# An encoder layer on one core: loads around the out projection spread, the second product's block split early, the sums of h given to GpSimd

## What is computed

```python
def encoder_layer(x, w_in, w_fourier, sink_logits, w_out, ln_mix_g, ln_mix_b, w_ff1, w_ff2, ln_ffn_g, ln_ffn_b):
    proj = x @ w_in
    ...
    heads = jnp.concatenate([fourier_mix(u, w_fourier),
                             windowed_attention(q, k, v, sink_logits)], axis=-1)
    x = layer_norm(DEEPNORM_ALPHA * x + heads @ w_out, ln_mix_g, ln_mix_b)
    h = jnp.square(jax.nn.relu(x @ w_ff1))
    x = layer_norm(DEEPNORM_ALPHA * x + h @ w_ff2, ln_ffn_g, ln_ffn_b)
    return x
```

## Time and profile before

| | before |
|---|---|
| median of three runs | 2422.47 us |
| the profiled execution | 2422.82 us, span 2421.2 us |
| TensorE busy | 2362.3 us (98%) |
| VectorE busy | 1568.6 us (65%) |
| ScalarE busy | 1101.7 us (46%) |
| GpSimd busy | 182.9 us (8%) |
| out projection | about 622 to 862 us of the span |
| up projection, groups 0, 1, 2 | 863.7, 1099.4 and 1336.1 us to 1649 us |

### The profile page before, as it was taken

One profiled execution on the slowest core, in us unless ns is written; L12 is line 12 of the kernel. 1 busy time (PEld: TensorE's weight loads), 2 busy tenths in 40 slices (PEclk: granted clock), 3 DMA queues, 4 the chain that ended last, 5 costly groups with the idle time before them and its releaser, 6 DMA issues. The chain is left out here.

```text
span 2421.2 us, 34853 instructions
## 1 busy us (share of the span) xinstructions
PE 2362.3 (98%) x12028; PEld 2065.8 (85%) x12028; DVE 1568.6 (65%) x2206; ACT 1101.7 (46%) x1819; POOL 182.9 (8%) x245
## 2 busy tenths in 40 slices
PE   7999999999999899999999999999999999999998
PEld 6888887999888789999999788888888888888887
DVE  8555366765666587786666655556566866774557
ACT  4111146887211155556555544445444444443333
POOL 2000001221223200000000000000000100000002
PEclk9999999999999999999999999999999999999999
DMA  8766766223466666677677755558877797787663
GB/s 302 285 266 228 272 203 223 79 65 90 137 217 217 248 257 259 239 272 279 232 262 262 281 209 199 199 199 306 277 227 216 259 306 226 210 273 264 192 193 120
DMA packets 220608, 547.85 MB, mean 226 GB/s; under 512 B 21704, under 2 KB 90952, under 8 KB 200908
## 3 DMA queue, kind: packets, MB, share of 16 engines
q1 hardware_dynamic: 204416, 488.19, 58.0%
q0 software_dynamic: 16080, 58.20, 7.6%
HBM read 365.95 MB, written 180.36 MB: 226 GB/s over the span
## 5 line engine op out<-in xcount | busy, mean ns | idle before, releaser
L71 PE MATMUL e_bank<-e_hi,e_lo 128*128 128x512 f32 x1120 | 435.8, 389 | 0.1
L73 PE MATMUL e_bank<-e_hi 128*128 128x512 f32 x1120 | 435.7, 389 | 0.0
L72 PE MATMUL e_bank<-e_lo,e_hi 128*128 128x512 f32 x1120 | 435.7, 389 | 0.0
L2353 DVE TENSOR_TENSOR e_lo<-e_raw,e_hi 128x896 fp32r<-128x896 f32 (+1 forms) x168 | 189.9, 1135 | 127.0 <-ACT e_hi L2308 126.7
L2308 ACT CAST e_hi<-e_raw 128x896 fp32r<-128x896 f32 (+1 forms) x168 | 165.2, 983 | 204.0 <-PE e_bank L73 196.8
L71 PEld LDWEIGHTS e_bank<-e_hi,e_lo 128*128 128x128 f32 x1120 | 210.3, 188 | 44.4 <-DVE e_lo L2353 1.0
L73 PEld LDWEIGHTS e_bank<-e_hi 128*128 128x128 f32 x1120 | 210.3, 188 | 43.7
L72 PEld LDWEIGHTS e_bank<-e_lo,e_hi 128*128 128x128 f32 x1120 | 210.3, 188 | 43.6
L71 PE MATMUL u_bank<-u_x_hi,u_wa_lo 128*128 128x384 f32 (+1 forms) x576 | 207.4, 360 | 4.0 <-ACT c_vt_raw L2055 3.6
L71 PE MATMUL u_bank<-u_x_hi,u_wb_lo 128*128 128x384 f32 (+1 forms) x576 | 203.4, 353 | 5.1 <-DVE u_x_first L1883 3.6
L73 PE MATMUL u_bank<-u_x_hi,u_wa_hi 128*128 128x384 f32 (+1 forms) x572 | 205.9, 360 | 0.0
(11 more groups left out here) (332 smaller groups left out, 4888.5 us busy)
## 6 DMA issues: line engine op xcount, KB each, us to landing
u_w_sum<-s_ws SPq DMA_DIRECT2D x33, 1024.0 KB, 4.8
c_vt_raw<-w_ff SPq DMA_DIRECT2D x24, 1024.0 KB, 7.0
c_q_raw<-w_ff SPq DMA_DIRECT2D x24, 1024.0 KB, 7.3
s_h<-c_k_raw SPq DMA_DIRECT2D x32, 768.0 KB, 6.7
e_raw<-s_t SPq DMA_DIRECT2D x96, 256.0 KB, 3.8
e_raw<-s_h SPq DMA_DIRECT2D x112, 192.0 KB, 2.8
ab_place<-w_ff SPq DMA_DIRECT2D x18, 1024.0 KB, 8.2
s_h<-c_k_raw SPq DMA_DIRECT2D x96, 192.0 KB, 2.7
```

The source lines that it names most:

```text
L71: tensor.matmul(out, w_lo, m_hi, start=first, stop=False, skip_group_check=again)
L72: tensor.matmul(out, w_hi, m_lo, start=False, stop=False, skip_group_check=again)
L73: return tensor.matmul(out, w_hi, m_hi, start=False, stop=last, skip_group_check=again)
L2353: dve.tensor_tensor(part(lo, n), part(raw, n), part(hi, n).bitcast(F32), ALU.subtract).then_inc(split, 1)
```

## The change

1. **Loads.** SyncE loads the first block of weight sums at n = 13, into a piece of memory that is free by then, and the two raw blocks at n = 15 and n = 17. GpSimd loads the four x blocks one by one at n = 10 to 13.
2. **The second product's block.** Of the weight sums, the columns of S2 (P6 of pair 0 reads them) are split in the out projection: one CAST more in ScalarE (128x512), one subtraction more in VectorE. P6 of pair 0 no longer waits for `wa_split`; P5 does. ScalarE's CASTs of the second side (`wb_high`) stand behind the copy of P1, and behind a wait for P6.
3. **The sums of h.** `h_sums` goes from VectorE to GpSimd, instruction for instruction, drains included. GpSimd now runs through the pairs; the x blocks with None are issued ahead of the sums in pair 11 of a group, all others behind the sums in pair 15.
4. **Code.** The loop of each group is one turn (two pairs) shorter, and two more pairs are written out.

```diff
@@ mix_out
+                if n == 13:
+                    sp.dma_start(w_sum, ws_d[0:P, :]).then_inc(w_sum_ld, 16)
+                if n in (15, 17):
+                    load_w_first(sp, n // 2 - 7)
...
+                if n == 10:
                     for s in range(2):
                         pool.wait_ge(mixed_st[s], 32)
-                    load_x_first(pool)
+                if 10 <= n < 10 + X_FIRST:
+                    load_x_first(pool, n - 10)
...
-            act.copy(wa_first_hi, w_raw_first[:, 0:512]).then_inc(wa_first_done, 1)
+            act.copy(wa_first_hi, w_raw_first[:, 0:512])
+            act.wait_ge(w_sum_ld, 16)
+            act.copy(wa_first[:, 0, 1, :], w_sum[:, 512:1024]).then_inc(wa_first_done, 1)
...
+                    dve.tensor_tensor(wa_first[:, 1, 1, :], w_sum[:, 512:1024], wa_first[:, 0, 1, :].bitcast(F32), ALU.subtract)
@@ mlp_up
-                with eng.Fori(1, NP // 2 - 2) as i:
+                with eng.Fori(1, NP // 2 - 3) as i:
...
+            def load_x(g, j):
+                freed = X_FREED[g][j] if g else None
+                if g:
+                    pool.wait_ge(prod_done, (g * NP - 5) * NPROD if freed is None else (g * NP - 1) * NPROD + freed + 1)
...
+            def body(g, p, s, start, end):
+                n = g * NP + p
+                early = g < LAST and isinstance(p, int) and p == NP - 5
+                if early:
+                    if g == 0:
+                        pool.wait_ge(mix_st[1], 16 * (NT // 4))
+                    for j in range(NPROD):
+                        if X_FREED[g + 1][j] is None:
+                            load_x(g + 1, j)
+                if not start or g:
+                    h_sums(n - 1, UP_GROUPS[g - 1 if start else g][1])
+                if end and g < LAST:
+                    for j in range(NPROD):
+                        if X_FREED[g + 1][j] is not None:
+                            load_x(g + 1, j)
...
-                if not start or g:
-                    h_sums(n - 1, UP_GROUPS[g - 1 if start else g][1])
                 if g == 0 and not start and not end:
                     w_sums(n + 1, 1 - s, isinstance(p, int) and p == 1)
...
                 if start and g == 0:
+                    act.wait_ge(prod_done, 2)
+                    wb_high(0, 0, w_sum_first)
                     act.copy(late[:, X_SLOT["T1"], :], bank[:, 1, 2, :])
...
-            wb_high(0, 0, w_sum_first)
             pairs(act, body)
...
                     elif prod == "P6":
                         if start and g == 0:
-                            pe.wait_ge(wa_split, 1)
                             pe.wait_ge(c_read[11], 1)
```

More of the change, by code:

```diff
@@ L1597, in _ @@
             x_high_first(2)
-            act.wait_ge(w_sum_ld, 16)
-            act.copy(wa_hi_sum, w_sum[:, 0:2 * 512])
+            act.copy(wa_hi_third, w_sum[:, 0:512])
         @block.vector
@@ L1740, in mlp_up @@
         al = Phase(nc, ctx, "u", held)
-        x_first, w_raw, x_first_ld, w_ld, (p1, u3, c22, h, h_sum), w_sum_ld, mix_st, x1_st, bank, (x_hi_first, w_sum_first, wa_hi_first, late) = first
+        x_first, w_raw, x_first_ld, w_ld, (p1, u3, c22, h, h_sum), w_sum_ld, mix_st, x1_st, bank, (x_hi_first, w_sum_first, wa_hi_first, s2_first, late) = first
         x_rest = al.sb("x_rest", [P, X_ARENA - X_FIRST * 1536])
@@ L1773, in pairs @@
                 body(g, 1, 1, False, False)
-                with eng.Fori(1, NP // 2 - 2) as i:
+                with eng.Fori(1, NP // 2 - 3) as i:
                     for s in range(2):
                         body(g, i * 2 + s, s, False, False)
-                for p in range(NP - 4, NP - 1):
+                for p in range(NP - 6, NP - 1):
                     body(g, p, p % 2, False, False)
@@ L1865, in _ @@
         def _(pool):
-            for g in range(len(UP_GROUPS)):
+            def load_x(g, j):
+                freed = X_FREED[g][j] if g else None
+                if g:
+                    pool.wait_ge(prod_done, (g * NP - 5) * NPROD if freed is None else (g * NP - 1) * NPROD + freed + 1)
                 q = first_pair(g)
-                if g < 2:
-                    pool.wait_ge(mix_st[g], 16 * (NT // 4))
-                for j in range(0 if g else X_FIRST, NPROD):
-                    if g:
-                        freed = X_FREED[g][j]
-                        pool.wait_ge(prod_done, (g * NP - 5) * NPROD if freed is None else (g * NP - 1) * NPROD + freed + 1)
-                    pool.dma_start(x_slot(g, j, False).rearrange("p q k c -> p q (k c)"),
-                                   xb_d[q:first_pair(g + 1), :, j, :].rearrange("q p c -> p q c")).then_inc(x_ld[j], 16)
+                pool.dma_start(x_slot(g, j, False).rearrange("p q k c -> p q (k c)"),
+                               xb_d[q:first_pair(g + 1), :, j, :].rearrange("q p c -> p q c")).then_inc(x_ld[j], 16)
@@ new lines, in h_sums @@
+            def h_sums(n, w):
+                for c in h_done:
+                    pool.wait_ge(h_done[c], n + 1)
+                pool.wait_ge(h_sum_st, 16 * n + 16)
+                pool.tensor_tensor(h_sum[:, 0, 0:w], h[:, 0, 1, 0:w], h[:, 1, 1, 0:w], ALU.add)
+                pool.tensor_tensor(h_sum[:, 2, 0:w], h[:, 0, 0, 0:w], h[:, 0, 1, 0:w], ALU.subtract)
+                pool.drain()
+                pool.tensor_tensor(h_sum[:, 1, 0:w], h_sum[:, 0, 0:w], h[:, 0, 0, 0:w], ALU.subtract)
+                pool.drain()
+                pool.tensor_tensor(h_sum[:, 3, 0:w], h[:, 1, 0, 0:w], h_sum[:, 1, 0:w], ALU.subtract
+                                   ).then_inc(h_summed, 1)
@@ L1878, in _ @@
+            pool.wait_ge(mix_st[0], 16 * (NT // 4))
+            for j in range(X_FIRST, NPROD):
+                load_x(0, j)
+            pairs(pool, body)
         @block.vector
@@ L1942, in body @@
                     x_low(g, 2)
+                    wa_low_third()
                     x_low(g, 3)
@@ L2122, in body @@
                     elif prod == "P5":
+                        if start and g == 0:
+                            pe.wait_ge(wa_split, 1)
                         pe.wait_ge(c_done[12], n + 1)
@@ L2138, in body @@
                                                                                      wa_lo[:, s, i, cols])
-                        if start and g == 0 and not side:
+                        if start and g == 0 and a in ("A12", "S1"):
                             hi = wa_hi_first[:, i - 1, cols]
+                        elif start and g == 0 and a == "S2":
+                            hi, lo = s2_first[:, 0, cols], s2_first[:, 1, cols]
                         mm = split_mm(pe, out, hi, lo, x_slot(g, j, True)[:, :, k, :],
```

44 lines of the change are left out of this document (14 added, 30 removed).

## The result

The changed kernel takes 2438.56 us (median of six, 2436.92 to 2440.66), the kernel before 2423.01 on the same chip (six, 2421.66 to 2426.85): ratio 1.0063, 95% interval 1.005 to 1.0076. The forecast was 2428.0, its range 2417.5 to 2437.0.

The account below looks back on a forecast made before the run. TensorE, busy 98% of the time, was taken to bound the kernel. Terms of -0.5 (border), +5.1 (group 0) and +1.2 (changes of group) made +5.8 us on the 2422.47 median: 2428 us, range 2417.5 to 2437.

Parts of the forecast that it names:

- the term for the changes of group: Changes to groups 1 and 2: later x loads against VectorE's freed time, net +0.6 us each, between -2 and +4.
- the one for group 0: Up projection, group 0: GpSimd's slower sums of h make P3 late, +5.1 us in all.
- The loads of the out projection end no wait of TensorE in the timeline there, so spreading them is worth 0.: Out projection: spreading the loads was to change the time by 0.
- Worth: -0.5 us: Border to the up projection: with the early split P7 starts at 871.0, not 871.4; -0.5 us.
- I take 0.90: Each GpSimd sum of h was to take 0.90 us, between 0.39 and 0.97; four make 3.6 us.
- P3 ... is about 0.2 us late: Plain pairs of group 0: a later relu delays C22 and so P3 by 0.2 us; nine pairs make 1.8 us.
- The five others: Pairs 1, 2 and 12 to 14 of group 0: VectorE has no gap; 0.6 to 0.7 us each, 3.3 us.
- it costs 0: Pairs of groups 1 and 2: U3 waits for P7, not for GpSimd's sums, so moving them costs 0.
- I take 1 us of loss: Changes of group: x loads issued behind their pair's sums were to lose 1 us at each change.
- More code written out: 0, fetched ahead.: Two more pairs written out outside the loops: the code is fetched ahead, 0.
- Much slower: VectorE goes first: Rival: VectorE's queued operations pass ahead of GpSimd's sums, 14 pairs lose 0.7 us more each, 2438 us; chance 0.07.
- Late loads: Rival: x blocks land 3 us late at both changes of group, +6 in place of +1.2, 2433 us; chance 0.07.

Follow-up runs that it names:

- run 1: Kernel before with only the spread loads and the early split of the second product's block, sums of h left on VectorE: 2410.95 us.
- run 10: Kernel before with only the out projection's loads of x and of the weights spread, no early split: 2412.16 us.
- run 11: Kernel before with only the four x loads on GpSimd's queue spread, the weight loads kept together: 2411.53 us.
- run 3: Changed kernel with GpSimd's two drains inside the sums replaced by waits on a semaphore that the sums raise: 2425.55 us.
- run 4: Changed kernel with the early x loads of pairs 11 and 27 issued behind that pair's sums, drains kept: 2431.22 us.
- run 5: Changed kernel with semaphore waits for GpSimd's drains, and the sums of pairs 15 and 31 back on VectorE: 2418.93 us.
- run 9: Changed kernel with semaphore waits for GpSimd's drains, and pairs 6 to 15 of each group written out: 2425.28 us.
- run 13: Changed kernel without drains, sums of pairs 15 and 31 on VectorE, ScalarE's rounding of the weights ahead of the relu in group 0: 2411.62 us.

## Why the prediction was wrong

The forecast was 10 us too low. Two of its terms stood at 0 and were far from it, the spread loads (-10.8 us measured) and the drains that moved with the sums (+12.2 us); the term for the changes of group stood at +1.2 us and measured +6.8; the one for group 0 stood at +5.1 and measured +8.3.

**"The loads of the out projection end no wait of TensorE in the timeline there, so spreading them is worth 0."** Wrong, and the largest error: runs 1, 10 and 11 give 11 to 12.5 us. The row at 804.79 was in the trace of before, 8.73 us with ScalarE's 17.03 us on the heads' load behind it. I had taken it for a wait at the stage's start. The load that hurt was another than the one that waited: x delayed the heads. The time from issue to landing says so, 22.4 us for the heads' load in place of 9.9; the share of the DMA engines doesn't, since it is about 1.00 from 780 to 795 in both kernels.

**"Worth: -0.5 us"** for the border was right: 19.11 to 18.57, and 19.12 to 18.56 between runs 10 and 1. P6 began at clock 1.00, and P7 waited as foreseen, 10.96 us behind the last transposes (860.28), where the forecast had 10.9.

**"I take 0.90"** for a sum: 1.01 alone, above my upper end of 0.97. An estimate by the Trainium skill (GPSIMD Engine Reference, "Elementwise — side-by-side cycle accounting") was 0.84; the measurement decides. That the two engines take turns was right; it shows in every plain pair of group 0.

**"P3 ... is about 0.2 us late"**, the right chain, with a term mis-sized. I had the relu at 8.86 us into the pair, `wa_low_raw` at 10.26 and the end of C22 at 12.60; without drains they are at 9.32, 10.79 and 13.13. The last sum ends 0.47 us later than I had it: VectorE passes ahead of the first sum, and a sum is 0.1 us longer. The slack was gone, so all of it arrived, seven times: 5.7 us where nine plain pairs were to give 1.8. The five others gave 2.5, not 3.3. Together with pair 10's 0.15, 8.3 us against 5.1.

**Groups 1 and 2, "it costs 0"**: right, but for pairs 27, 30 and 31.

**The term that was missing.** I cost the sums and the loads of GpSimd one by one, and the drain between the sums not at all: pairs 11 and 27 are 12.3 us longer, and 12.2 of these went with the drains (run 3; run 4 shows where they come from). Of a moved step every instruction counts, the drains too. On VectorE, which issues no load, the same drains left no such gap.

**"Net +0.6 each"** at the changes of group: +3.9 and +3.0. The delay of the loads was about right (first one "near 1092", 7.7 us into its pair; it came at 8.1). Wrong was "I take 1 us of loss": ScalarE stood for the block for 5.06 us, and the loads alone (run 5) are 5.3 and 3.0 us. VectorE's gain in the pair is 0.65 us at the first change; the 0.3 at the second is inside the scatter of pair 32.

So against +5.8: -10.8 and -0.5, then +8.3, +12.3, +6.8, -0.6 and +0.7, which is +16.2. The two missed terms are of opposite sign and about equal. That is luck: a forecast 10 us off looks better than its working was.

**"More code written out: 0, fetched ahead."** Written out, pairs 10 and 11 lose 0.15 us each; the loop's pairs lose 0.8 (runs 3 and 9). So the term was a small gain, and no run here shows how code is fetched.

**What the rivals had.** "Much slower: VectorE goes first" gave 2438, nearly the measured number, by luck: its sum has neither the drains nor the spread loads; its mechanism is there in the loop (run 9) at 0.7 us in seven pairs. "Late loads" had +6 for the changes of group, and 6.8 was measured.

## What to carry to other kernels

Ask of each load that is moved not only who waits for it but what else it delays: compare the time from issue to landing of the loads behind it, not only the share of the DMA engines. On GpSimd, order dependent instructions by a semaphore where the engine also issues loads, and put no sums ahead of a load that someone needs. When work goes to a slower engine, look at who waits for its end and what stands behind that wait on the third engine: one CAST moved ahead gave 6.9 us, while VectorE's freed time gave nothing in the plain pairs, where TensorE is busy without a gap (run 13 is level with run 1).
